# Turning y and the attention probabilities by transposing DMA transfers instead of on TensorE, in a two-block fp32 kernel

## What is computed

```python
u = rms_norm(h, norm_mix[layer])
proj = u @ w_in[layer]
z, xbc, dt_raw, q, k, v, g_ssd, g_attn = jnp.split(proj, IN_SPLITS, axis=-1)
y_ssd = ssd_mixer(z, xbc, dt_raw, ...)       # y * silu(z), rms over each of 4 groups, times norm_w
y_attn = dilated_attention_mixer(q, k, v, cos, sin)   # 8 heads, three patterns each
merged = (jax.nn.sigmoid(g_ssd) * (y_ssd @ w_ssd_branch[layer])
          + jax.nn.sigmoid(g_attn) * (y_attn @ w_attn_branch[layer]))
h = h + merged @ w_out[layer]
u = rms_norm(h, norm_ffn[layer])
gate, up = jnp.split(u @ w_gate_up[layer], 2, axis=-1)
h = h + (jax.nn.silu(gate) * up) @ w_down[layer]
```

## Time and profile before

| what | us |
|---|---|
| median of the runs | 1545.76 |
| the profiled execution | 1546.51 |
| its span | 1544.7 |
| PE busy | 1526.3 (99% of the span), 7734 matmuls |
| DVE busy | 1021.0 (66%) |
| ACT busy | 924.0 (60%) |
| POOL busy | 79.1 (5%), 55 instructions |
| DMA | 280.09 MB, mean 181 GB/s |

### The profile page before, as it was taken

One profiled execution on the slowest core, in us unless ns is written; L12 is line 12 of the kernel. 1 busy time (PEld: TensorE's weight loads), 2 busy tenths in 40 slices (PEclk: granted clock), 3 DMA queues, 4 the chain that ended last, 5 costly groups with the idle time before them and its releaser, 6 DMA issues.

```text
span 1544.7 us, 19149 instructions
## 1 busy us (share of the span) xinstructions
PE 1526.3 (99%) x7734; PEld 1288.4 (83%) x7734; DVE 1021.0 (66%) x1324; ACT 924.0 (60%) x1114; POOL 79.1 (5%) x55
## 2 busy tenths in 40 slices
PE   7999999999999999999999999999999999999998
PEld 7888888888888888988888888888888878888887
DVE  5978776646665554787886665566555576677665
ACT  5766777474355553667677566436555465656564
POOL 1000000000001000000000000000110020002000
PEclk9999999999999999999999999999999999999999
DMA  7455554554457675445555464446767575437541
GB/s 272 165 172 156 178 167 174 168 181 156 148 210 222 204 217 199 164 159 163 171 178 170 169 173 170 163 165 207 216 189 235 211 250 187 149 137 244 178 148 71
DMA packets 100399, 280.09 MB, mean 181 GB/s; under 512 B 65079, under 2 KB 66008, under 8 KB 69848
## 3 DMA queue, kind: packets, MB, share of 16 engines
q1 hardware_dynamic: 99208, 276.44, 53.8%
q10 hardware_dynamic: 1104, 2.43, 0.4%
HBM read 261.69 MB, written 1.84 MB: 171 GB/s over the span
## 4 chain that ended last, share of the span: by engine, by line
PE 86%; DVE 6%; ACT 4%; issue 3%; DMA 0%; ACTq 0%; DVEq 0%
PE ps L641 23%; PE ps L643 23%; PE ps L642 23%; PE ps L646 3%; DVE w_low L1640 2%; PE ps L911 2%; PE ps L912 2%; PE ps L913 2%; ACT w_high L1154 2%; PE ps L774 2%; DVE conv L1726 1%; DVE scratch L1931 1%; PE ps L818 1%; PE ps L749 0%; PE ps L779 0%
## 5 line engine op out<-in xcount | busy, mean ns | idle before, releaser
L1640 DVE TENSOR_TENSOR w_low<-w_raw,w_high 128x2048 fp32r<-128x2048 f32 (+1 forms) x250 | 566.7, 2267 | 410.1 <-ACT w_high L1154 343.3
L641 PE MATMUL ps<-w_high,u_high 128*128 128x512 f32 x1376 | 547.6, 398 | 0.5 <-DVE w_low L1640 0.5
L1154 ACT ACTIVATE w_high<-w_raw 128x2048 fp32r<-128x2048 f32 (+1 forms) x196 | 369.2, 1884 | 288.7 <-PE ps L643 275.3
L643 PE MATMUL ps<-w_high,u_low 128*128 128x512 f32 x1376 | 536.9, 390 | 0.0
L642 PE MATMUL ps<-w_low,u_high 128*128 128x512 f32 x1376 | 536.1, 390 | 0.0
L643 PEld LDWEIGHTS ps<-w_high,u_low 128*128 128x128 f32 x1376 | 258.2, 188 | 55.1
L641 PEld LDWEIGHTS ps<-w_high,u_high 128*128 128x128 f32 x1376 | 258.6, 188 | 54.6 <-issue 1.9
L642 PEld LDWEIGHTS ps<-w_low,u_high 128*128 128x128 f32 x1376 | 258.7, 188 | 53.0 <-issue 1.9
L641 PE MATMUL ps<-w_high,b_high 128*128 128x512 f32 x384 | 152.2, 396 | 0.0
L643 PE MATMUL ps<-w_high,b_low 128*128 128x512 f32 x384 | 149.8, 390 | 0.0
L642 PE MATMUL ps<-w_low,b_high 128*128 128x512 f32 x384 | 149.6, 390 | 0.0
(11 more groups left out here) (236 smaller groups left out, 1430.8 us busy)
## 6 DMA issues: line engine op xcount, KB each, us to landing
w_raw<-in_stream SPq DMA_DIRECT2D x238, 1024.0 KB, 4.9
w_raw<-in_stream SPq DMA_DIRECT2D x12, 512.0 KB, 4.1
par<-in_pars SPq DMA_DIRECT2D x4, 269.0 KB, 5.2
h<-in_x SPq DMA_DIRECT2D x4, 256.0 KB, 5.1
ple_gain<-in_ple_g ACTq DMA_DIRECT2D x2, 512.0 KB, 5.2
out<-h SPq DMA_DIRECT2D x4, 256.0 KB, 2.0
scratch<-in_const SPq DMA_DIRECT2D x1, 768.0 KB, 7.4
rev<-scratch ACTq DMA_DIRECT2D x1, 768.0 KB, 3.6
```

The lines of the kernel that those rows point to most:

```text
L641: nc.tensor.matmul(o, hi, whi, start=start, stop=False, **kw)
L643: return nc.tensor.matmul(o, lo, whi, start=False, stop=stop, **kw)
L1154: nc.scalar.activation(WH[:, c % RING, 0:n], W[:, c % RING, 0:n], ACT.Copy).then_inc(high_ready, 1)
L1640: return nc.vector.tensor_tensor(out=o, in0=a, in1=b, op=op)
```

## The change

For each of the four groups, y is turned by a transfer. After DVE's scaling POOL splits the words (new `y_half`), SP issues the transposing transfer at its turn 2i+16, POOL puts the words together again and writes the turned y over y itself; DVE's multiplication by the gain, now from SBUF, and the split into `b_high` and `b_low` come at 2i+16 instead of 2i+15. For seven of the eight heads (all but the last) POOL splits the probabilities (`lay_apart`), SP issues a transfer at s+6, POOL puts them together in `pT` (`put_together`), PE multiplies with the values at s+4 instead of s+3, in bank 7 (the seventh head in bank 4), and the output is split at s+6 instead of s+5. The eighth head keeps PE's transposes and its places.

```diff
@@ -517,10 +526,14 @@
+        QK_TURN, Y_TURN = (0, 2, 4, 6, 8, 9, 10), (1, 3, 5, 7)
+        Y_WEIGH = 16
         HEAD_AT = (36, 38, 40, 42, 48, 50, 52, 54)
+        O_AT = tuple(s + 6 - (s == 54) for s in HEAD_AT)
+        O_BANK = (7, 7, 7, 7, 7, 7, 4, 6)
@@ -562,10 +575,30 @@
+            def turn_y(l, c):
+
+                for g, i in enumerate(XT):
+                    m = Y_TURN[g]
+                    if c == 2 * i + 16:
+                        if g == 2:
+                            sp.wait_ge(xt_ps.sem, xt_ps.at(l, GROUPS))
+                        sp.wait_ge(words_split.sem, words_split.at(l, m + 1))
+                        sp.dma_start_transpose(y_back[g].rearrange("p (m r) -> p m r", r=P), y_half[g])\
+                            .then_inc(words_turned[m % 2].sem, 16)
+
+            def turn_p(l, c):
+
+                for n, s in enumerate(HEAD_AT[:7]):
+                    if c == s + 6:
+                        sp.wait_ge(p_split.sem, p_split.at(l, n + 1))
+                        sp.dma_start_transpose(p_back[n // 4][:, :, :], p_half[n // 4][:, :, :].rearrange("p h k n -> p (h k n)"))\
+                            .then_inc(p_turned.sem, 16)
...
+            def weigh_values(n):
+                b, v = O_BANK[n], vv[n // 4][:, :, tok(n % 4)]
+                nc.tensor.matmul(ps[:, b, 0:S], v[:, 0], pT[:, 0:S], start=True, stop=False)
+                nc.tensor.matmul(ps[:, b, P:S], v[:, 1], pT[:, S:S + P], start=False, stop=True).then_inc(o_ps.sem, 1)
@@ -754,22 +794,10 @@
-                    if c == 2 * i + 13:
-                        pe.wait_ge(y_scaled.sem, y_scaled.at(l, g + 1))
...
-                        for t in range(T):
-                            for j in range(4):
-                                last = turn(ps[:, 4 + t, tok(j)], Y[g % 2][:, t, tok(j)])
-                            last.then_inc(yt_ps.sem, 1)
...
@@ -802,22 +828,22 @@
-                    if c == s + 2:
-                        pe.wait_ge(att_p.sem, att_p.at(l, n + 1))
-                        if n:
-                            pe.wait_ge(pt_out.sem, pt_out.at(l, n))
+                    if n < 7 and c == s + 4:
+                        pe.wait_ge(pt_out.sem, pt_out.at(l, n + 1))
+                        if n == 6:
+                            pe.wait_ge(att_masked.sem, att_masked.at(l, 8))
+                        elif n:
+                            pe.wait_ge(o_ready.sem, o_ready.at(l, n))
+                        weigh_values(n)
+                    if n == 7 and c == s + 2:
+                        pe.wait_ge(att_p.sem, att_p.at(l, 8))
+                        pe.wait_ge(o_ready.sem, o_ready.at(l, 6))
                         turn(ps[:, 7, tok(0)], sc0[:, tok(0)])
                         turn(ps[:, 7, tok(1)], sc1[:, tok(0)])
                         turn(ps[:, 7, tok(2)], sc1[:, tok(1)]).then_inc(pt_ps.sem, 1)
...
@@ -1320,33 +1348,34 @@
+                    for n in range(8):
+                        if c == O_AT[n]:
+                            act.wait_ge(o_ps.sem, o_ps.at(l, n + 1))
+                            nc.scalar.activation(bH[:, 16 + n, :], ps[:, O_BANK[n], 0:S], ACT.Copy).then_inc(o_high.sem, 1)
...
@@ -1599,16 +1628,53 @@
+                def lay_apart(n):
+
+                    pool.wait_ge(att_p.sem, att_p.at(l, n + 1))
+                    if n == 4:
+                        pool.wait_ge(qk_out.sem, qk_out.at(l, 6))
+                    half = p_half[n // 4][:, :, :, :]
+                    nc.gpsimd.tensor_copy(half[:, :, 0, :], sc0[:, tok(0)].bitcast(U16).rearrange("p (n h) -> p h n", h=2))
+                    nc.gpsimd.tensor_copy(half[:, :, 1:, :].rearrange("p h k n -> p h (k n)"),
+                                          sc1[:, 0:S].bitcast(U16).rearrange("p (n h) -> p h n", h=2)).then_inc(p_split.sem, 1)
+
+                def put_together(n):
+
+                    pool.wait_ge(p_turned.sem, p_turned.at(l, 16 * (n + 1)))
+                    if n:
+                        pool.wait_ge(o_ps.sem, o_ps.at(l, n))
+                    nc.gpsimd.tensor_copy(pT.bitcast(U16).rearrange("p (n h) -> p h n", h=2),
+                                          p_back[n // 4][:, :, :].rearrange("p (h k) n -> p h (k n)", h=2)).then_inc(pt_out.sem, 1)
+
                 for n in range(7):
+                    if n == 4:
+                        lay_apart(0)
+                        put_together(0)
+                        lay_apart(1)
+                    if n >= 5:
+                        put_together(n - 4)
+                        lay_apart(n - 3)
                     pool.wait_ge(roped.sem, roped.at(l, n + 1))
...
+                    if n < GROUPS:
+                        g, m = n, Y_TURN[n]
+                        pool.wait_ge(y_scaled.sem, y_scaled.at(l, g + 1))
+                        if g == 2:
+                            pool.wait_ge(qk_out.sem, qk_out.at(l, 3))
+                        nc.gpsimd.tensor_copy(y_half[g].rearrange("p (h n) -> p h n", h=2),
+                                              words_of(Y[g % 2]).rearrange("p n h -> p h n")).then_inc(words_split.sem, 1)
+                        pool.wait_ge(words_turned[m % 2].sem, words_turned[m % 2].at(l, 16 * (m // 2 + 1)))
+                        nc.gpsimd.tensor_copy(words_of(Y[g % 2]).rearrange("p n h -> p h n"),
+                                              y_back[g].rearrange("p (h m) -> p h m", h=2)).then_inc(y_whole.sem, 1)
+                put_together(3)
+                for n in range(4, 7):
+                    lay_apart(n)
+                    put_together(n)
...
@@ -1893,14 +1959,14 @@
-                        if c == 2 * i + 15:
+                        if c == 2 * i + Y_WEIGH:
+                            dve.wait_ge(y_whole.sem, y_whole.at(l, g + 1))
                             for t in range(T):
-                                dve.wait_ge(yt_ps.sem, yt_ps.at(l, 2 * g + t + 1))
-                                tt(four(ev[0][:, t, :]), four(ps[:, 4 + t, :]),
+                                tt(four(y[:, t, :]), four(y[:, t, :]),
                                    bc(par[:, C_SN + 4 * g:C_SN + 4 * g + 4].unsqueeze(2), 4, P), ALU.mult).then_inc(y_weighted.sem, 1)
```

More of the change, by code:

```diff
@@ L247, in build @@
                    early("qk_turned6", 1, 20, 2 * T * 512, U16)[:, :]]
+        y_half = [words("y_halves0", E_AT, [2 * T * 512])[:, :], words("y_halves1", E_AT, [2 * T * 512])[:, :],
+                  words("y_halves2", E_AT, [2 * T * 512])[:, :], words("y_halves3", BTOK_AT, [2 * T * 512])[:, :]]
+        y_back = [words("y_turned0", Q_AT + 1024, [2 * T * 512])[:, :], words("y_turned1", Q_AT + 1024, [2 * T * 512])[:, :],
+                  early("y_turned2", 0, 20, 2 * T * 512, U16)[:, :], early("y_turned3", 0, 20, 2 * T * 512, U16)[:, :]]
         pT = E0[:, 1152:1536]
+        p_half = [words(f"p_halves{i}", (Y_AT + 1024, BTOK_AT + 1024)[i], [2, T + 1, P]) for i in range(2)]
+        p_back = [words(f"p_turned{i}", (Y_AT + 1408, BTOK_AT + 1408)[i], [2 * (T + 1), P]) for i in range(2)]
         V0 = cut(2048)
@@ L369, in build @@
         off_ps = signal("off_ps", GROUPS)
-        yt_ps = signal("yt_ps", 2 * GROUPS)
         qk_ps = signal("qk_ps", 1)
-        qk_split = signal("qk_split", 7)
-        qk_turned = [signal("qk_turned0", 16 * 4), signal("qk_turned1", 16 * 3)]
+        words_split = signal("words_split", 7 + GROUPS)
+        words_turned = [signal("words_turned0", 16 * 6), signal("words_turned1", 16 * 5)]
+        y_whole = signal("y_whole", GROUPS)
         score_ps = signal("score_ps", 8)
-        pt_ps = signal("pt_ps", 8)
+        pt_ps = signal("pt_ps", 1)
+        p_split = signal("p_split", 7)
+        p_turned = signal("p_turned", 16 * 7)
         o_ps = signal("o_ps", 8)
@@ L591, in _ @@
                     turn_qk(l, c)
+                    turn_y(l, c)
+                    turn_p(l, c)
                     if l == 0 and c == 2:
@@ L811, in before @@
                         turn(ps[:, 7, tok(2)], sc1[:, tok(1)]).then_inc(pt_ps.sem, 1)
-                    if c == s + 3:
-                        pe.wait_ge(pt_out.sem, pt_out.at(l, n + 1))
-                        if hh < 3:
-                            pe.wait_ge(att_masked.sem, att_masked.at(l, n + 2))
-                        elif n:
-                            pe.wait_ge(o_ready.sem, o_ready.at(l, n))
-                        nc.tensor.matmul(ps[:, 6, 0:S], vv[n // 4][:, 0, tok(hh)], pT[:, 0:S], start=True, stop=False)
-                        nc.tensor.matmul(ps[:, 6, P:S], vv[n // 4][:, 1, tok(hh)], pT[:, S:S + P], start=False,
-                                         stop=True).then_inc(o_ps.sem, 1)
+                    if n == 7 and c == s + 3:
+                        pe.wait_ge(pt_out.sem, pt_out.at(l, 8))
+                        weigh_values(n)
                 if c == OUT_AT:
@@ L1340, in _ @@
                                 .then_inc(att_exp.sem, 1)
-                    for n, s in enumerate(HEAD_AT):
-                        if c == s + 4:
```

(11 more changed lines are left out.)

50 lines of the change are left out of this document (23 added, 27 removed).

## The result

| | before | after |
|---|---|---|
| median, us (4 runs each) | 1545.7 | 1533.1 (1532.54 to 1534.16) |
| ratio, 95% interval | | 0.9916 [0.9905, 0.9928] |
| profiled execution: time, span | 1546.51, 1544.7 | 1532.54, 1530.7 |
| PE busy, matmuls | 1526.3, 7734 | 1510.8, 7628 |
| DVE, ACT, POOL busy | 1021.0, 924.0, 79.1 | 1043.2, 919.3, 178.5 |

The change takes 12.6 us off, 11.1 to 14.7 by the interval; 12.3 was forecast. The spans (1544.68 and 1530.74 with their hundredths) differ by 13.9, but 1.0 of that comes from the loads at the start: the subtraction `w_low` that starts at 35.70 before starts at 34.68 after. I therefore measure each kernel **from this `w_low` to the end of the span** (the *body*): 1509.0 before, 1496.1 after, a gain of 12.9.

The account below looks back on a forecast made before the run. PE, busy 99%, was taken to bound the kernel. Gains of 7.0 + 4.8 + 6.7 = 18.5 less losses of 3.6 and 2.6 made -12.3 us, from 1545.76 to 1533.4, range 1526 to 1542.5.

Parts of the forecast that it names:

- What bounds the kernel: PE, busy 99%: other engines' gains or losses count only where PE comes to wait for them.
- The transposes: PE's transposes of y and of 14 heads' probabilities go: 7.0 and 4.8 us gained.
- the stall: PE's wait for ACT's copy of the turned probabilities before the product with the values: 14 x 0.48 = 6.7 us gained.
- The rival that halves these: transposes save half of 11.8 and the stall the booked 3.3: 1542.8 us, 8%.
- Chunk 47: PE's turn of the last q tile waits 1.8 us for the fourth head's output to be read; 3.6 lost in two layers.
- The shift of PE by head 3's product: the product (0.57 us) now in chunk 46 brings PE to chunk 47's transposes at 327.5 instead of 326.90.
- Chunks 21 and 27: y's weighing on DVE, moved ahead of chunks 20 and 26, makes PE wait 0.4 and 0.7 us; 2.6 lost in all.
- Covered costs: transfers landing within 8.8 us and POOL's copies finish before PE's need: 0.6 us spare at chunk 32, 2.3 at heads; no cost.
- Rival 3: POOL's copies hold up DVE's chains before chunks 21, 27 and 32, 1.25 to 1.89 us each: 1543.0 us, 16%.
- Rival 5: transfers land too late at chunk 32 and seven heads; a landing of 11.7 us eats the gain, 13 gives 1567; 7%.

Follow-up runs that it names:

- Runs 1 to 3: the changed kernel with run 1's edit, with run 2's edit, and with both together: 1529.49, 1530.22 and 1528.01 us.
- run 1: the changed kernel with ACT's split of the heads' outputs moved ahead of the merges of q and k: 1529.49 us.
- run 2: the changed kernel with the weighing of y back at chunk 2i+15 for all groups but group 2: 1530.22 us.
- run 9: the changed kernel with POOL's copy that puts a head's probabilities together done twice instead of once: 1533.53 us.
- run 10: the changed kernel with POOL's split of the words of two tiles of q done four times instead of once: 1549.94 us.
- run 8: the changed kernel with POOL's split of the words of two tiles of q done seven times instead of once: 1570.55 us.
- Run 6: the changed kernel with POOL's copy that puts a head's probabilities together done four times instead of once: 1544.07 us.
- run 7: the changed kernel with POOL's copy that puts a head's probabilities together done nine times instead of once: 1608.89 us.
- Run 4: the kernel before with only the y part of the change, the probabilities still turned on TensorE: 1543.38 us.
- run 5: the kernel before with only the heads' part of the change, y still turned on TensorE: 1539.96 us.

## Why the prediction was right

- *What bounds the kernel.* Right: DVE is busy 22 us more and POOL 99, and the time follows PE's program and its waits alone.
- *The transposes* (7.0 and 4.8) and *the stall* (6.7): measured 7.0, 4.7 and 7.0 by the ledger. Reading the stall from the timeline, not from the wait view's 0.24, was the right choice: after, all products but one stand at 0.66 or 0.67, and 0.48 a head came back. The rival that halves these is out. Runs 1 to 3 leave the gains by themselves: 19.1, where 18.5 stood in the prediction.
- *Chunk 47* (3.6): measured 3.8, and run 1 gives back 3.8. The shift of PE by head 3's product was needed; without it 2.4 a layer would have stood there.
- *Chunks 21 and 27* (2.6): measured 2.4, and run 2 gives back 2.4. That the sum is so near is in part luck: the prediction has waits of 0.4 and 0.7 and 0.2 more for PE's being early; measured are two waits of 0.40, and each costs 0.6. One name in this step was wrong: the row that ends at 151.31 is not the convolution's last step but the sum that ends the state space's part and frees banks 4 and 5. The times argued from are those of the right row, since PE waits for just that.
- *Covered costs.* Right in that none was paid. But I put 8.8 in for every landing, and y's took 4.8 at most and the probabilities' 7.3; the spare at the heads was 2.8 to 9.3, not 2.3. Where it is 2.8, one extra copy used it up (run 9).
- *Rival 3, contention.* It did not happen, for want of copies in these places: POOL's copies of y end at 126.8, before chunk 20. Where contention did happen it did not reach PE: beside the copy back at 124.09 DVE's column of 0.17 took 2.53. The price of 1.25 to 1.89 for a copy beside such a chain holds: with three more copies a place costs 4.5 and with six 9.2 (runs 10 and 8), 1.5 a copy, what the clock adds included.
- *Rival 5, the late transfer.* The point at which it decides was argued with a price of 1 us per us of wait. Run 6 shows 4.9 for 3.2, run 7 some 21 on top of 54.7: the clock. In run 6 copies of 3.3 more for each head, partly held up by DVE, take 11.3 of the 12.9, so the change was nearer to this point than its landings of 5.2 to 7.3 for the heads, against the 11.7 of my sum, suggest.
- *Parts.* The prediction treated gains as plain sums and followed the moved weighing at chunks 20, 26 and 32, not at chunk 38. Run 4 shows that the y part by itself is worth 2.8 and not 4.6, and its rows put this down to the weighing there, which makes ACT late for head 0's product: a wait that the other part removes. That the whole came out well rests on both parts being there.

## What to carry to other kernels

In a kernel that one engine fills, price a step by the starts around it, against a chunk that lacks it; then walk each moved instruction along its engine's order and ask which wait of the full engine it now stands ahead of. Such waits, once found, are mended by order alone: two edits without a new instruction took 6.2 us off on top of the 12.9 of the change itself. An instruction moved on another engine can delay a chain on which the full engine waits a chunk later, so a part can be worth less alone than beside the edit that moves that wait.

## What the runs showed of the hardware

- A wait of PE costs more than its length where the clock drops behind it. After the 1.71 at chunk 47 the windows show 1.00; behind 3.22 there is a stretch of 0.67. In the wait of 6.15 (run 8) the clock is down already before the wait ends, at 0.69 on average, and the 6.2 us behind it, to 155.6, are at 0.50 (1.2 GHz); the step of 2.7 took 12.2. In run 10 waits of 1.25 and 1.84 ahead of the thin products of 64 columns were followed by 4 and 8 us at 0.57 in layer 0, while the same wait of 1.25 at the same place of layer 1 left the clock at 1.00 and cost 1.5. So length alone does not decide; what does was not settled. In run 5 it fell to 0.72 with no wait of PE, behind matmuls after which the kernel before kept 1.00.
- DVE and POOL hold each other up by whole instructions: POOL's copy of 256 columns, 0.40 by itself, took 2.4 behind `w_low` at 11 of 14 heads of the changed kernel, and DVE's pair took 4.67 for 1.29.
- The transposing transfer of the same 0.5 MB landed in 4.3 to 4.8 for y and in up to 9.8 for q and k; the slow ones are issued right behind a load (at 137.65 behind one whose issue ends at 137.60), the fast ones some us later.
